# Third expert weight loaded from ScalarE's DMA queue, first and second from SyncE's, in a two-layer mixture-of-experts trunk

## The reference, cut to what matters

```python
def expert_block(args):
    tok, gate, e = args
    h = xf[tok]
    y = (jax.nn.silu(h @ w1[e]) * (h @ w3[e])) @ w2[e]
    return y.astype(F32) * gate[:, None]
```

## Time and profile before

| | us |
|---|---|
| Median of 3 timed runs | 2444.59 (2442.73 to 2445.73) |
| Profiled execution, its own time | 2440.64 |
| Span of the profiled execution, first to last instruction | 2438.5 |

### The profile page before, as it was taken

One profiled execution on the slowest core, in us unless ns is written; L12 is line 12 of the kernel. 1 busy time (PEld: TensorE's weight loads), 2 busy tenths in 40 slices (PEclk: granted clock), 3 DMA queues, 4 the chain that ended last, 5 costly groups with the idle time before them and its releaser, 6 DMA issues. The chain is left out here.

```text
span 2438.5 us, 31605 instructions
## 1 busy us (share of the span) xinstructions
PE 2185.7 (90%) x10840; PEld 1588.3 (65%) x10840; DVE 1610.5 (66%) x2260; ACT 1354.0 (56%) x1754; POOL 543.2 (22%) x310
## 2 busy tenths in 40 slices
PE   6999999799998998998679999997989899989956
PEld 5788756576676766665266886565766676766632
DVE  2583323588888877886545923246978788878847
ACT  3534631387777767676034355215867777767731
POOL 0001000242343333332000010003433333333310
PEclk9899999899999999999789999998999999999988
DMA  6213040699999999996721230408999999999965
GB/s 192 77 44 147 1 169 26 191 353 338 343 347 337 349 333 349 339 332 246 293 85 52 65 127 1 177 18 282 356 339 343 346 346 337 348 341 327 341 232 244
DMA packets 141434, 580.22 MB, mean 238 GB/s; under 512 B 40292, under 2 KB 65124, under 8 KB 88856
## 3 DMA queue, kind: packets, MB, share of 16 engines
q1 hardware_dynamic: 96280, 511.73, 58.3%
q0 software_dynamic: 45056, 67.22, 8.9%
HBM read 555.19 MB, written 61.37 MB: 253 GB/s over the span
## 5 line engine op out<-in xcount | busy, mean ns | idle before, releaser
L1193 POOL DMA_INDIRECT y_rows<-y,index x128 | 290.6, 2271 | 822.6 <-ACT y L1424 796.1
L1246 PE MATMUL ps_up<-w_hi,rowsT_hi 128*100 128x512 f32 x1024 | 422.0, 412 | 27.9 <-issue 19.0
L1248 PE MATMUL ps_up<-w_hi,rowsT_lo 128*100 128x512 f32 x1024 | 405.4, 396 | 0.0
L1390 ACT CAST w_hi<-w_other 128x2048 fp32r<-128x2048 f32 x128 | 245.7, 1920 | 184.7 <-DMA w_other<-exp_w 171.5
L1390 ACT CAST w_hi<-w 128x2048 fp32r<-128x2048 f32 x128 | 245.2, 1917 | 150.8 <-DMA w<-exp_w 87.0
L1327 DVE TENSOR_TENSOR w_lo<-w,w_hi 128x2048 fp32r<-128x2048 f32 x128 | 292.2, 2284 | 27.6 <-ACT w_hi L1390 27.5
L1327 DVE TENSOR_TENSOR w_other_lo<-w_other,w_hi 128x2048 fp32r<-128x2048 f32 x128 | 292.0, 2282 | 6.8 <-ACT w_hi L1390 6.7
L1271 PE MATMUL ps_y<-w_hi,hiddenT_hi 128*100 128x512 f32 x512 | 214.2, 418 | 74.3 <-issue 70.2
L1185 POOL DMA_INDIRECT rows<-x_rows,index x128 | 202.2, 1580 | 334.0 <-DVE index L1312 278.4
L1246 PEld LDWEIGHTS ps_up<-w_hi,rowsT_hi 128*100 128x100 f32 x1024 | 173.9, 170 | 86.0 <-issue 33.6
L1332 DVE TENSOR_TENSOR w_lo<-w,w_hi 128x2048 fp32r<-128x2048 f32 x96 | 219.1, 2283 | 2.7 <-ACT w_hi L1397 2.7
(11 more groups left out here) (228 smaller groups left out, 4135.6 us busy)
## 6 DMA issues: line engine op xcount, KB each, us to landing
w<-exp_w SPq DMA_DIRECT2D x232, 1024.0 KB, 15.1
w_other<-exp_w SPq DMA_DIRECT2D x128, 1024.0 KB
w_first<-exp_w SPq DMA_DIRECT2D x34, 1024.0 KB, 9.2
got<-y_rows SPq DMA_DIRECT2D x8, 4096.0 KB, 12.8
wbuf<-w_in SPq DMA_DIRECT2D x16, 1024.0 KB, 5.6
w_out_sb<-w_out SPq DMA_DIRECT2D x2, 4096.0 KB, 19.2
bias<-bias_tiles SPq DMA_DIRECT2D x2, 2560.0 KB, 9.0
sh_w<-sh_w SPq DMA_DIRECT2D x4, 1024.0 KB, 9.0
```

Source lines behind the costliest of these rows:

```text
L1193: pool.indirect_dma_start(d["y_rows"], bass.IndirectOffsetOnAxis(ap=index[0:CAP, x.step, 1:2], axis=0), y[0:CAP, x.slot, :], None, bounds_ ...
L1246: pe.matmul(ps_up[b][0:CAP], hi, w_hi, start=(k == 0), stop=False)
L1248: mm = pe.matmul(ps_up[b][0:CAP], lo, w_hi, start=False, stop=(k == KD - 1))
L1390: act.copy(w13_hi[:, :, k, :], w13[x.slot][:, :, k, :]).then_inc(S["up_hi_b" if half else "up_hi_a"], 1)
```

## The change

The w2 load leaves SyncE's program, with its wait for `down_made`. ScalarE's program gets `dn_load`: three loads (experts 1, 2, 3) ahead of its first cast, and in every turn x from 1 to 60 one load, of expert x+3, right behind `scaled(x-1)`. `scaled(x-1)` itself waits for `down_made` of expert x-1, whose slot expert x+3 takes over, so no new wait is written. SyncE's up loads keep their wait for `up_made`; the first of them keeps the wait for `dma_turns`, which ScalarE's loads don't have.

```diff
@@ -1150,7 +1150,7 @@
             @block.sync
             def _(sp):
-                (w1, w3), w2d = _expert_weights(d)
+                w1, w3 = _expert_weights(d)[0]
                 sp.wait_ge(S["dma_turns"], 3)
...
-                    if x.has(-SLOTS):
-                        sp.wait_ge(S["down_made"], x.n - SLOTS + 1)
-                    if x.has(-1):
-                        sp.dma_start(w2[x.slot], w2d[e].rearrange("o p j c -> p (o j) c")).then_inc(S[f"dn{x.slot}_in"], 16)
-
                 _laps(sp, load)
...
+                w2d = _expert_weights(d)[1]
+
+                def dn_load(x):
+
+                    e = bass.ds(l * NE + x.n, 1)
+                    act.dma_start(w2[x.slot], w2d[e].rearrange("o p j c -> p (o j) c")).then_inc(S[f"dn{x.slot}_in"], 16)
+
...
+                for k in range(1, SLOTS):
+                    dn_load(Turn(0, k))
                 up_hi(Turn(0, 0), 0)
...
                     if x.has(-1):
                         scaled(x + -1)
+                        if x.has(SLOTS - 1):
+                            dn_load(x + (SLOTS - 1))
```

## The result

The changed kernel took **2450.59 us** (median of 10 runs, 2446.26 to 2458.39), the kernel before, on the same chip, 2441.39 us (10 runs). The ratio is **1.0045**, with a 95% interval of 1.0030 to 1.0059: slower by 7 to 14 us. In a second comparison it was 1.0056 (1.0035 to 1.0076). The time lies inside the predicted range, but 5.6 us above the forecast of 2445 and on the other side of the 0.2% that counts as no change. The size is that of rival B. B had named the first gather of a block; that the gathers of all later turns would be waited for, no rival had said.

The account below looks back on a forecast made before the run. Two lagging DMA engines were taken to bound the expert blocks. Per layer -4.05 (start) + 4.3 (order) = +0.25, so +0.5 on 2440.64 gave 2441.1 profiled, plus 3.95 for the timed median: 2445 us, range 2428 to 2457.

Parts of the forecast that it names:

- rival B: Block start and turns: early w2 loads gain nothing, w2 overtakes in full; +9 to +12 us, 2454 to 2457; chance 0.17.
- The bound: Expert blocks: two lagging DMA engines of sixteen pace every cast, so their work sets the block's length.
- the second queue adds no bandwidth: DMA engines: one hardware queue already brings 426 GB/s, all that sixteen such engines can do.
- rival A: Turns: a second hardware queue makes the lagging engines faster; 2414 to 2432, gain capped at 62 us a layer; chance 0.18.
- the tail with a share of 0.13: Both block ends: two engines still move loads alone, for less than the 8 us or so of before.
- I take it that the two never run dry between the first load and the last: Expert block: the two lagging engines always have queued work, so a load's issue time doesn't matter while they are fed.
- SyncE's earlier issue: SyncE's up loads, freed of the wait for `down_made`, go out 3 to 4 us earlier; worth nothing.
- ScalarE's issues: ScalarE's turns: an address step and issue, about 0.5 us, fit its idle time or cover; worth nothing.
- The start term: Block start: the first three w2 loads start 4.05 us sooner; -4.05 us a layer, between 0 and -4.05.
- another 1 to 2 us there are absorbed: Block start: TensorE's extra wait for the first gather costs nothing, the lagging engines setting the block's length.
- The order term: Lagging engines: w2 on its own queue overtakes up loads; +4.3 us a layer, between 0 and +6.2.
- The predicted loss in the last turns: Block end: w2(62) and part of w2(63) are served before up(62); +3.1 and +1.2, in all +4.3 us a layer.

Follow-up runs that it names:

- e2: The kernel before, with only the first three w2 loads of each block issued by ScalarE at the start, later ones on SyncE: 2448.80 us, ratio 1.0038.
- e4: Apparently (label not given there) the changed kernel with GpSimd issuing the gather of x+3 before the scatter of x-2: 2450.05 us, ratio 1.0051.
- after_again: The changed kernel unaltered, run and profiled a second time beside others on one chip: 2453.57 us, ratio 1.0056 to the kernel before.
- e5: The changed kernel with its first three w2 loads of each block back on SyncE, later ones on ScalarE: 2453.01 us, ratio 1.0061.
- e3: The kernel before, all loads on SyncE's one queue, with the up loads of expert x+1 issued before w2 of expert x: 2432.59 us, ratio 0.9973.
- e7: The kernel before, one queue, up loads of expert x+2 issued before w2 of x: 2425.71 us, ratio 0.9952; second run 2422.69 us, 0.9940.
- e9: The kernel before, one queue, each gather fetching only 50 of an expert's 100 rows, computation left out: 2313.09 us, ratio 0.9482.

## Why the prediction failed where it did

That the time fell inside the range is luck. The forecast was the difference of two terms; one had the wrong sign, the other stood on a wait that vanished.

**The bound: right for before, lost after.** In the kernel before two engines lag, and ScalarE waits for them. The length of the turns hardly tells who is the bound: the 55 turns after the ninth output of layer one take 584.8 us before and 588.4 in `e2`, and with two queues from 581.9 (`e4`) to 592.4 (`after_again`). That the second queue adds no bandwidth was right as well, and rival A fell: 340 GB/s at 900 to 1000 in both kernels. But the prediction said that if the tail with a share of 0.13 were missing, its reading of the bound had failed. It is missing. "I take it that the two never run dry between the first load and the last" holds for the kernel before only; in the changed one they run dry at 480 and again at the end: the last w2 load, issued at 1123.27, is in by 1128 with no tail behind it.

**SyncE's earlier issue, ScalarE's issues: nothing, as said.** `w2` still never waits, and ScalarE has its pair of instructions done in its idle time. Neither was measured alone.

**The start term failed in sign.** The step was: "the two lagging engines get a start of 4.05 us". The loads did start (438 GB/s at 448). But the step looked at the first idle stretch and not at the next. Four slots were full and no further load could be issued before the first expert was done with its slot. And "another 1 to 2 us there are absorbed" was 5.5 us. TensorE did make them up in layer one of `e2` by the ninth output, but the loads did not: it is this very expert that frees the slot, so they lay idle meanwhile. Measured alone (`e2`) the term is +4.3 us a layer, not -4.05. Rival B had said that "the start brings nothing"; it costs.

**The order term: right sign, wrong road.** It said +4.3 us a layer, at most +6.2, because queues are served in turns and w2 overtakes up loads. Rings alone (`e5`) cost 15.2 us, 7.6 a layer; by the interval 4.8 to 10.0, so that the size doesn't exclude +6.2. The road does: the transfer overtaken is not the up load, whose waits went from 258.5 us to none, but the gather, whose waits went from 11.9 us to 108.5. Three queues are at work in the block, and I had priced only two. The gathers' 19.6 us in flight for 13.8 is 1.4 times. The Trainium skill, DMA: Bandwidth & Descriptors, section "Queues, rings and completion order", has an engine take turns between its queues packet by packet. By that rule GpSimd's queue had half of the turns and now has a third, and its part of the bytes in a round falls from 1.49 / (1.49 + 5.32) KB = 22% to 1.49 / (1.49 + 4.86 + 7.28) = 11%, an estimate from the mean packets of the whole program (by the page's packets and MB). The direction agrees with these rows; the size, 2 against 1.4, does not, and no row shows single packets.

The row that could have told was on the page: TensorE had already waited 5.67 us for a gather, and 11.9 us in three waits was all the margin that it lacked. I priced what a second queue does to the waits that were there (258.5 us, ScalarE's), and not what it does to the transfers that were just in time.

**The end of the block.** The predicted loss in the last turns (+4.3) did not come about as such. Up loads are in earlier, not later: there is no wait for them at all. In `e3` and `e7` the same idea, turned round on one queue, is worth 7.5 and 12 to 15 us. That is 3.8 a layer for one w2 load moved back and 6.1 to 7.4 for two, near the 3.1 for one that the prediction had. The price of an order was about right, and stood at the wrong place.

**What stays open.** The profiled executions of the two-queue kernels have a lower granted clock over the span, 0.938 to 0.945 against 0.955 to 0.960 with one queue. With the lighter gathers it is 0.961 with two queues and 0.963 with one, so it goes with the late gathers. Whether TensorE's slower columns cost time of their own, or fall in time that the loads pace anyway, was not separated. Nor was it tried to issue the gathers earlier by finding the token numbers earlier. How start and rings share the changed kernel's loss is known only to some 4 to 10 us, the width of the intervals.

## What to carry to other kernels

Where the DMA engines are the bound, as here, look for what a second hardware queue will delay: it brought no bandwidth, and the one that lost was a third queue, GpSimd's gathers, which had been just in time. Try the order of the loads on one queue first: here up loads in the order in which they are wanted (`e3`) gave 7.5 us, and two experts ahead of w2, past that order (`e7`), 12 to 15, where the second queue lost 9 to 16. Before pricing an earlier start, follow the slots: if the next load must wait for a buffer, the idle time only moves.

## What the runs showed of the hardware that I had not expected

**Fewer gathered rows took away far more time than their bytes explain.** A turn moves some 3.67 MB: three weights of 1.05 MB, and 67.22 MB / 128 of GpSimd's. How much the cut to 50 rows takes away depends on the count. The page's HBM reads fall from 555.19 to 528.98 MB, 0.2 MB a turn, which is 50 rows of 4 KB in every gather. The queue's own bytes fall from 67.22 to 59.51 MB, 0.06 MB a turn, and its packets from 45056 to 34816. The program tells why the two may differ: an expert has 64 tokens on average, and the numbers of rows without a token lie out of bounds. 128 x 2 x 64 rows of 4 KB are 67.1 MB, so the queue's count seems to be that of the rows that were moved, and the cut 1.6% of a turn and not 5.6%. It took 127 us off, 5.2% of the whole program (57 turns x 1.09 us x 2 layers would be 124), and 84% of the waits for up loads (258.5 to 40.6 us), and brought the turns to TensorE's own pace: at 900 to 1000 TensorE is busy for 98.07 us instead of 88.87, and the rate rises from 340 to 367 GB/s. Spread evenly over sixteen engines the bytes left out would be 12.8 KB each by the larger count, 0.5 us a turn at 26.5 GB/s, and 3.8 KB or 0.14 us by the smaller; about 1.1 us a turn went away. So gathers cost more than their bytes, on the lagging engines or on all; which, no run here tells. The lag itself is shorter, not gone: in `e9` the share is still 0.13 from 1066 to 1070, behind a last load issued at 1055.88, where it had been 0.13 for some 7 us before. The Trainium skill, same page, section "Latency and other measured facts", guesses that fetching software descriptors crowds two engines; this pair agrees with its direction, and neither the engines' numbers nor the fetches are in the rows.

**ScalarE's queue runs ahead of its engine.** An issue of w2 that stands behind the scaling in the program goes out before it. Timeline of ScalarE, changed kernel:

```profile
615.66 0.34 ACTq L1392 DMA_DIRECT2D w_first<-exp_w  x1
616.32 1.13 ACT L1426 ACTIVATE y<-ps_y,gate 100x1024 f32<-100x1024 f32 x1
```

The load goes out 0.66 us before the activation ahead of it has begun, and the engine loses nothing to it.
